# A mixture-of-experts encoder step on one core: 32 instead of 16 tokens in the second gather tile, planned up-projection steps, gates stored by block

## The reference, cut to what matters

```python
s = einsum('thpd,hpnd->thpn', q, sub_keys)          # 8 heads, 2 x 128 keys
s_top, i_top = top_k(s, 16)
cand = s_top[:, :, 0, :, None] + s_top[:, :, 1, None, :]
f_s, f_pos = top_k(cand, 16)                         # 8 x 16 = 128 experts of 128 x 128 for each token
g = softmax(f_s)
act = gelu(einsum('thkd,td->thk', peer_u[e_idx], x))
out = einsum('thk,thkd->td', g * act, peer_v[e_idx])
```

## Time and profile before

| | us |
|---|---|
| median of 3 runs | 1941.97 (1940.36 to 1944.2) |
| the profiled execution, its own time | 1945.57 |
| its span, first to last instruction | 1943.5 |
| TensorE busy in it | 1853.2 (95%) |
| VectorE busy | 1446.0 (74%) |
| ScalarE busy | 763.3 (39%) |

### The profile page before, as it was taken

How to read it: one execution, slowest core, us unless ns; L and a number is a source line. 1 busy time by engine, 2 the same in 40 slices (tenths; PEclk the granted TensorE clock), 3 DMA queues, 4 the chain that set the end, 5 groups by cost and what they waited for, 6 DMA issues and landing times.

```text
span 1943.5 us, 27288 instructions
## 1 busy us (share of the span) xinstructions
PE 1853.2 (95%) x10187; PEld 1690.9 (87%) x10187; DVE 1446.0 (74%) x2723; ACT 763.3 (39%) x1193; POOL 521.8 (27%) x372
## 2 busy tenths in 40 slices
PE   7899988898999999999999999989999999999994
PEld 1799745495999999999999999979999999999994
DVE  3586544426888688899799898877777777777776
ACT  2332243315223333356547767623333333333332
POOL 1124110102230121234234343452222223223222
PEclk9899986898999999999999999999999999999997
DMA  7443100314224588789979999999999999999971
GB/s 267 166 161 104 55 17 2 113 61 131 76 65 130 181 256 246 233 270 326 316 232 336 317 325 325 331 387 375 344 330 334 343 338 330 345 343 336 333 242 71
DMA packets 192671, 461.26 MB, mean 237 GB/s; under 512 B 16560, under 2 KB 104640, under 8 KB 188832
## 3 DMA queue, kind: packets, MB, share of 16 engines
q1 hardware_dynamic: 148912, 300.41, 46.2%
q0 software_dynamic: 43632, 159.17, 23.1%
HBM read 399.19 MB, written 59.85 MB: 236 GB/s over the span
## 4 chain that ended last, share of the span: by engine, by line
PE 87%; DMA 4%; DVE 4%; ACT 2%; issue 1%; POOL 1%; SPq 0%; POOLq 0%; DVEq 0%; ACTq 0%
PE ps L575 86%; DMA gath<-peer_u,routed 3%; DMA ada_w<-ada 1%; ACT prob L987 1%; DVE gath L1751 1%; PE ps L791 0%; POOL act_lo L510 0%; ACT act_hi L987 0%; DVE stats L1817 0%; PE ps L613 0%; DMA silu_row<-c_row 0%; DVE prob L1500 0%; POOL w_lo L503 0%; DVE y_tok L1811 0%; DVE tmp L1430 0%
## 5 line engine op out<-in xcount | busy, mean ns | idle before, releaser
L987 ACT ACTIVATE w_hi<-w_raw 128x1024 fp32r<-128x1024 f32 (+1 forms) x303 | 319.2, 1054 | 774.6 <-PE ps L575 754.1
L575 PE MATMUL ps<-act_hi,w_hi 128*128 128x432 f32 (+1 forms) x1752 | 594.6, 339 | 12.2 <-issue 4.3
L575 PE MATMUL ps<-act_lo,w_hi 128*128 128x432 f32 (+1 forms) x1752 | 584.9, 334 | 0.0
L575 PE MATMUL ps<-act_hi,w_lo 128*128 128x432 f32 (+1 forms) x1752 | 584.8, 334 | 0.0
L1623 DVE TENSOR_TENSOR w_lo<-w_raw,w_hi 128x1024 fp32r<-128x1024 f32 x256 | 313.2, 1224 | 209.4 <-ACT w_hi L987 206.1
L575 PE MATMUL ps<-ga_hi,w_hi 128*128 128x432 f32 x1024 | 367.0, 358 | 7.9 <-DVE ga_lo L1745 7.9
L575 PE MATMUL ps<-ga_lo,w_hi 128*128 128x432 f32 x1024 | 366.7, 358 | 0.0
L575 PE MATMUL ps<-ga_hi,w_lo 128*128 128x432 f32 x1024 | 366.5, 358 | 0.0
L563 POOL DMA_INDIRECT gath<-peer_u,routed x144 | 226.4, 1572 | 489.3 <-DVE act_v L1751 386.9
L575 PEld LDWEIGHTS ps<-act_hi,w_hi 128*128 128x128 f32 x1752 | 333.5, 190 | 22.2 <-issue 4.3
L575 PEld LDWEIGHTS ps<-act_lo,w_hi 128*128 128x128 f32 x1752 | 333.6, 190 | 7.7
(11 more groups left out here) (251 smaller groups left out, 1767.1 us busy)
## 6 DMA issues: line engine op xcount, KB each, us to landing
w_raw<-peer_uT SPq DMA_DIRECT2D x128, 512.0 KB, 4.7
w_raw<-peer_v SPq DMA_DIRECT2D x128, 512.0 KB, 5.9
early_activations<-e_out SPq DMA_DIRECT2D x128, 216.0 KB, 5.3
dense_gates<-piece SPq DMA_DIRECT2D x27, 1024.0 KB, 6.6
a_in<-early_activations SPq DMA_DIRECT2D x128, 216.0 KB, 6.2
g_in<-dense_gates SPq DMA_DIRECT2D x48, 576.0 KB, 8.0
w_raw<-w_in SPq DMA_DIRECT2D x17, 512.0 KB, 4.3
ada_w<-ada SPq DMA_DIRECT2D x16, 512.0 KB, 17.1
```

The lines of the kernel that those rows point to most:

```text
L575: return nc.tensor.matmul(out, lhsT, rhs, start=start, stop=stop)
L987: return nc.scalar.activation(out, in_, func, **kw)
```

## The change

- `EX` is 32: 416 tokens are dense, 32 are in the second gather tile (4 ranks of 32 slots), and there are 128 + 32 = 160 gathers from each table. 26 pieces and 52 pair steps are left.
- `plan()` replaces `STAGES` and `gathered`. It goes through the steps 0 to 127 with an estimated DVE budget for each, puts as many pieces of `choose` into a step as fit, may place a pair and a piece of `choose` in the same step, and spreads the dots evenly from step 13 up to step 124. `SLOTS_TO` spreads the 160 `peer_v` rows evenly over steps 130 to 254.
- Gates of both groups of a pair are multiplied on ACT (`times_gate(g)` and `times_gate(g + 1)`); the DVE half is gone.
- `dense_gates` is laid out by block of eight expert blocks. `store_piece` now writes 16 runs of 512 bytes for each of 128 partitions, `load_gates` reads one run of 6656 bytes for each partition, in `PARTS` = 2 DMAs.

```diff
-EX = 16
+EX = 32
...
-PARTS = 3
+PARTS = 2
...
+CHUNK_WORK = (26, 11, 22, 16, 14, 22, 33, 23, 29, 30, 23, 32)
+CHUNKS = len(CHUNK_WORK)
+LOW_WORK, DOT_WORK, HOTS_WORK = 12, 13, 25
+BLOCK_TIME, ROWS_TIME = 47 * ND // 432, 18
+CHOOSE_ORDER = (NPT - 1, LAST, 0, 1, 2)
...
+LAST_DOT = NB - 4
+def share(n, of):
+    return min(NG, NG * n * (n + 4 * of) // (5 * of * of))
+def plan():
+    chunks, rows, dots = {t: [] for t in CHOOSE_ORDER}, {}, []
+    queue = [(t, w) for t in CHOOSE_ORDER for w in CHUNK_WORK]
+    groups = [(t, g) for t in range(NPT - 1) for g in range(PTILES[t][0] // TOK, min(sum(PTILES[t]), ND) // TOK, 2)]
+    spare, first_dot = 0, None
+    for c in range(NB):
+        left = spare + BLOCK_TIME - LOW_WORK
+        if groups and len(chunks[groups[0][0]]) == CHUNKS and c >= chunks[groups[0][0]][-1] + 3 and (c % 3 or not queue):
+            rows[c] = groups.pop(0)[1]
+            left += ROWS_TIME - HOTS_WORK
+        if first_dot is None and len(chunks[CHOOSE_ORDER[0]]) == CHUNKS:
+            first_dot = chunks[CHOOSE_ORDER[0]][-1] + 3
+        had = dots[-1] if dots else 0
+        done = had if first_dot is None or c < first_dot else share(c - first_dot + 1, LAST_DOT - first_dot + 1)
+        left -= DOT_WORK * (done - had)
+        dots.append(done)
+        while c >= AHEAD and queue and 2 * left >= queue[0][1]:
+            t, w = queue.pop(0)
+            chunks[t].append(c)
+            left -= w
+        spare = min(left, 20)
...
+SLOTS_TO = [min(NG, NG * max(0, c - SLOTS_FROM + 1) // (2 * NB - 1 - SLOTS_FROM)) for c in range(2 * NB)]
...
-        gates = nc.dram_tensor("dense_gates", (NPIECE, P, NK, GS), F32, kind="Internal").ap()
+        gates = nc.dram_tensor("dense_gates", (NK // IBLK, P, NPIECE, IBLK * GS), F32, kind="Internal").ap()
...
-                sp.dma_start(gates[q], piece[:, q % 2]).then_inc(s_gw[q % 2], 16)
+                sp.dma_start(gates[:, :, q].rearrange("b j e -> j b e"), piece[:, q % 2].rearrange("j (b i) t -> j b (i t)", i=IBLK)).then_inc(s_gw[q % 2], 16)
...
-                src = gates[sub].rearrange("s j (b i) t -> b j s (i t)", i=IBLK)[k]
-                sp.dma_start(g_in[:, k % 2, sub].rearrange("p s i t -> p s (i t)"), src).then_inc(s_gi[k % 2], 16)
+                sp.dma_start(g_in[:, k % 2, sub].rearrange("p s i t -> p s (i t)"), gates[k, :, sub]).then_inc(s_gi[k % 2], 16)
...
-                if g % 2 == 0:
-                    pe.wait_ge(s["onej"], g // 2 + 1)
-                else:
-                    pe.wait_ge(s["onejd"], g // 2 + 1)
+                pe.wait_ge(s["onej"], g + 1)
...
                     times_gate(g)
+                    times_gate(g + 1)
...
-                dve.wait_ge(s["eqj"], g // 2 + 1)
-                gate = sel[:, 2, TOK * (g + 1):TOK * (g + 2)].unsqueeze(2).to_broadcast([P, TOK, NK])
-                v.tensor_tensor(one_j[:, (g + 1) % 4], one_j[:, (g + 1) % 4], gate, ALU.mult).then_inc(s["onejd"], 1)
```

More of the change, by code:

```diff
@@ L75 @@
 AB = 8
-PARTS = 3
+PARTS = 2
 UBANKS = 3
[L79 to L83, removed]
-AHEAD = 3
[L85 to L89, removed]
-    else:
[L91 to L94, removed]
@@ L95 @@
-ROUTED = _s
+CHUNK_WORK = (26, 11, 22, 16, 14, 22, 33, 23, 29, 30, 23, 32)
[3 more added lines that the diff above has]
+CHOOSE_ORDER = (NPT - 1, LAST, 0, 1, 2)
+NTH = {t: n + 1 for n, t in enumerate(CHOOSE_ORDER)}
+AHEAD = 3
+LAST_DOT = NB - 4
[22 more added lines that the diff above has]
+        spare = min(left, 20)
+    assert not queue and not groups and dots[-1] == NG
+    return chunks, rows, dots
@@ L96 @@
+CHUNK_AT, ROWS_AT, DOTS_TO = plan()
+ROUTED = max(ROWS_AT) + 1
 assert ROUTED <= NB - 8
-FIRST_DOT = AHEAD + CHUNKS + 2
 WEIGH_AT = NB
 SLOTS_FROM = WEIGH_AT + 2
-SHORT_CHUNKS = (0, 1, 2, 3, 4, 6, 7, 8, 10)
+DOTS_TO += [NG] * NB
+SLOTS_TO = [min(NG, NG * max(0, c - SLOTS_FROM + 1) // (2 * NB - 1 - SLOTS_FROM)) for c in range(2 * NB)]
 NEW_AT = (1, 2, 4, 6, 8)
[L105 to L115, removed]
@@ L118 @@
[L118 to L123, removed]
 assert DOTS_TO[WEIGH_AT - 1] == NG and SLOTS_TO[-2] == NG
@@ L275, in build @@
         expert, gate_s = routed[:, 0], routed[:, 1].bitcast(F32)
-        act_v = at("act_v", [P, NG], B + 113536)
-        act_g = at("act_g", [P, NG], B + 114112)
-        of_ex = at("of_ex", [P, EX], B + 114688)
+        act_v = at("act_v", [P, NG], B + 112384 + 8 * NG)
+        act_g = at("act_g", [P, NG], B + 112384 + 12 * NG)
+        of_ex = at("of_ex", [P, EX], B + 112384 + 16 * NG)
         f_ex = at("f_ex", [P, D], B + 12288)
@@ L314, in build @@
         assert 101376 + EB * ND * 4 <= 108288
-        assert base + B + 114752 <= 229344
+        assert base + B + 112384 + 16 * NG + 4 * EX <= 229344
         HI = (w3_hi[:], w_hi[:, 1], w_hi[:, 0])
@@ L355, in build @@
             mx ex pn pt pte pv pve rowsB rowr sqa sqb mhi mlo m mean1 rc1 sq1 var1 varr h2a x0g h2hi h2lo smm h2t
-            h2te gd wgt fsub fexp top1 chose selt sele onei eqj onej onejd gmat gst eg
+            h2te gd wgt fsub fexp top1 chose selt sele onei eqj onej gmat gst eg
             ga gahi galo fmm fe var2 std2 wsm ax ft r2 yt y yn yg rstd2 out nv otr ote""".split()
@@ L463, in _ @@
                     copy_h2()
-                if c == CHOOSE_AT[LAST] + CHUNKS + 6:
+                if c == CHUNK_AT[LAST][-1] + 7:
                     regroup()
@@ L930, in _ @@
                 for t in range(NPT - 1):
-                    if b == CHOOSE_AT[t] + CHUNKS:
+                    if b == CHUNK_AT[t][-1] + 1:
                         transpose_choices(t)
@@ L1254, in _ @@
                 for t in range(NPT):
-                    if c == CHOOSE_AT[t] + CHUNKS + 1 and t < NPT - 1:
+                    if c == CHUNK_AT[t][-1] + 2 and t < NPT - 1:
                         transposed(t)
-                    if c == CHOOSE_AT[t] + 6:
+                    if c == CHUNK_AT[t][4] + 1:
                         exponentials(t)
@@ L1774, in _ @@
                     dot(n)
-                if c == CHUNKS - 1:
+                if c == CHUNK_AT[NPT - 1][-1]:
                     dve.wait_ge(s["h2te"], 2)
@@ L1779, in _ @@
                 for t in range(NPT):
[L1780 to L1783, removed]
+                    for i, at_step in enumerate(CHUNK_AT[t]):
+                        if at_step == c:
+                            choosing = choose(t) if i == 0 else choosing
+                            next(choosing)
                 g = ROWS_AT.get(c)
```

## The result

The changed kernel takes 1894.88 us (median of 4 runs, 1890.76 to 1897.4) against 1941.3 before: the ratio is 0.9752, 95% interval 0.9738 to 0.9766. The prediction was 1892 us, range 1882 to 1912. The profiled execution took 1897.4 us with a span of 1895.3.

What follows compares the result with a forecast made beforehand. TensorE was taken as the bound, by number of matmuls times spacing. 42 + 3.6 + 9.9 - 5 = 50.5 us less took the profiled 1945.6 to 1895, or 1892 us against the median 1941.97; range 1882 to 1912.

Steps and rivals of the forecast that it cites:

- dense columns: Both projections: 16 fewer columns in each of 6144 matmuls, 6.8 to 6.9 ns each, 42 us less.
- pairs: Up-projection: two pair steps fewer, each costing 1.79 us of TensorE, 3.6 us less.
- hole and slow clock: Hand-over to the down-projection: evenly spread dots remove TensorE's 8.1 us gap and 1.8 us of slow clock, 9.9 us less.
- waits behind mixed steps: Steps with both a pair and a `choose` piece: late one-hots delay ACT's PSUM copies, TensorE waits; 5 us, bounds 0 to 19.
- The rival of the weight loads: Both projections: 188 ns weight loads set the pace, so fewer columns change nothing; 1934 us, chance 0.04.
- The forecast that they would be covered: Beside pairs and in the down-projection: transfers just keep up with TensorE, nothing added to the time.
- the limit by which I judged them: DMA share of 1.01 at 362 to 369 GB/s, the most any profiled window showed.
- the rival of the short stores: Pair steps: 512-byte gate stores pace them; chance 0.07 over 49 ns each (slower), 0.02 level, 0.09 between (1895 to 1937).
- the 17 us of bound on the down-projection: Down-projection: transfers could hold blocks to 4.65 us against 4.52, 17 us in all; nothing was added for it.
- landings of `dense_gates`: Sign against the forecast: gate loads landing far above 6.6 us, with ACT waiting for `piece` to be free.

Runs made afterwards that it cites:

- two experiments that cut different links: Changed kernel with VectorE building one-hots ahead of the `choose` piece: 1889.76 us; changed kernel with ScalarE's PSUM copies ahead of the gate products: 1887.99 us.

## Why the prediction was right

Term by term, from the profiled executions (the spans differ by 48.2 us; forecast 50.5):

| term | forecast | measured |
|---|---|---|
| dense columns | -42 | -43.3: 128 x (4.70 - 4.52) = 23.0 up, 600.6 - 580.3 = 20.3 down |
| pairs | -3.6 | -5.7: 54 x 1.79 - 52 x (6.27 - 4.52) |
| hole and slow clock | -9.9 | -10.4 (8.5 and 1.9) |
| waits behind mixed steps | +5 | +7.3, and +1.3 behind a gather that landed after 8.77 us (block 99) |
| the front part, noise | 0 | +0.9 |
| the end of the program | 0 | +2.6 |

**The columns.** 104.12 / 552 = 188.6 ns for a matmul over 416 columns, forecast 188.9. The slope between 288 and 432 columns was the right price. The rival of the weight loads is out: PEld is now busy 99.23 of 100 us with loads of the same 188 ns, and the spacing fell all the same. As it fell to just these 188 ns, the run with 64 tokens is the better proof: with the same loads of 188 ns its blocks start 4.16 us apart where nothing waits, 173 ns a matmul. The Trainium skill ("Perfetto Trace Analysis", Identifying the Most-Contended Engine) judges TensorE's headroom by the busy share of its weight loads, next to its share of the peak rate; the first does not tell it for this stream: 96 and 99% left room for the 3.6% that the columns gave.

**The hole.** Shown from both sides: spread dots close it in the old kernel, and in the new one it stays closed with the long loads. With shorter runs some of it is back, 1.9 us with the old layout and 5.3 with runs of 256 bytes, because the weight loads stand behind the issue of the gate loads. The prediction looked at a standing SP queue only behind the stores, where it is free, and did not see this part of what the new layout gives.

**Mixed steps.** The mechanism was right in each of its links (late one-hots, products in front of copies, the bank), and two experiments that cut different links show it. The size was 5 against 7.3 us. Every mixed step of the plan holds one dot, for which the prediction had 0.5 us; in the step shown above the one-hots of the pair start 0.8 us after the next block does, and that block takes 7.83 us in place of 6.27. The choice to cost ScalarE's extra products at nothing, since they fit a step that holds only a pair, was the weak place: they fit there, but in a mixed step they are what delays the copies, and 5 of the 7.3 us vanish when half of them go back (2.2 us are left). That cost stood inside the 5 us and was not seen as the price of this edit.

**Transfers.** The forecast that they would be covered was right; the limit by which I judged them was not one. A share of 1.03 at 389 GB/s held no one up in the changed kernel's hand-over, 1.09 at 360 GB/s did not with runs of 256 bytes, and 397 GB/s is reached with 64 tokens. The price of a short store was nearly right, 27.2 ns against 26. So the rival of the short stores was further from its point of decision than worked out, and the 17 us of bound on the down-projection were too careful. The forecast that landings of `dense_gates` would show it could not be used: the page has no landing times for them.

**The end.** GpSimd's last operation ends 8.5 us before the span does (1884.45 + 2.33 to 1895.3), 5.9 before the change. The prediction had no term for it. Its 2.6 us are more than the 2.3 by which the spans fall short of the forecast; that the larger waits are made up for by the columns and pairs is luck. The measured terms sum to -47.3; 0.9 us of the difference between the spans is left without a place.

## What to carry to other kernels

An engine that has room in each kind of step can still delay another in a step that mixes two: look at what stands behind a waiting instruction in its queue, and put what the bound engine needs next (here the copies that free a bank) ahead of it. Spread work that comes through a few buffers by the rate of those buffers, since a burst at the end of a stage becomes a hole for the engine that sets the time, and a slow clock after it. When TensorE sets the time and columns can be traded for gathers, go on until the next bound shows: another 32 tokens gave 48 us more. And look at what stands behind a load of many short runs in a DMA queue: here it was the weights that the bound engine needed next.

## What the runs showed of the hardware

- The DMA share of a window is no measure of a limit here: the down-projection with 256-byte runs held 1.09 for 400 us with TensorE busy for all of them. By the packet records beside pairs, packets of 256, 512 and 8192 bytes took 18.1, 27.2 and 310.5 ns: some 8 ns for each on top of its bytes (19.4 ns for 512).
- The issue of loads in many short runs can hold SP's queue: the first two gate loads at the hand-over took 0.85 us of issue with runs of 6656 bytes, 6.48 with 512 and 14.60 with 256, and the first weight load behind them started 10 and 17 us later than in the changed kernel. Later gate loads of the same kernels took about 0.5 us of issue each; why the first ones took so long is not shown.
- The end of the program went with the number of gathers, and not in proportion: from the end of GpSimd's last operation to the end of the span it takes 5.9 us with 288 gathers (before, and with 16 tokens), 8.5 with 320 and 4.7 with 384. Rows of the last operation, of the kernel with 32 and of that with 64 tokens (spans 1895.3 and 1849.8):

```profile
1884.45 2.33 POOL L572 TENSOR_TENSOR y_tok<-y_tok,gb 64x1024 f32<-64x1024 f32 x1 [1.16 <-DVE y_tok L1809]
```

```profile
1842.69 2.33 POOL L572 TENSOR_TENSOR y_tok<-y_tok,gb 64x1024 f32<-64x1024 f32 x1 [1.16 <-DVE y_tok L1811]
```

What GpSimd does in that time is not shown; the cause stays open.
